# Values and narrow columns of the first mixer in one projection of 304 columns

## The reference

```python
h = rms_norm(x, norm_mix)
proj = h @ w_in
(nsa_q, nsa_kc, nsa_vc, nsa_ks, nsa_vs, nsa_kw, nsa_vw, nsa_g,
 sb_q, sb_k, sb_v, gla_q, gla_k, gla_v, gla_a, gla_g,
 fox_q, fox_k, fox_v, fox_f, gate_logits) = jnp.split(proj, offsets, axis=-1)
...
g = jax.nn.sigmoid(gate_logits).reshape(B, S, G, HPG, 3)               # nsa_g, 24 columns
log_a = jax.nn.log_sigmoid(a_lr @ w_alpha + b_alpha) / GLA_TAU         # gla_a, 16 columns
log_f = jax.nn.log_sigmoid(f_logit + b_f)                              # fox_f, 8 columns
```

## Time and profile before

| | |
|---|---|
| three runs | 1696.88, 1697.82, 1698.09 us; median 1697.82 |
| profiled execution | 1696.86 us, span 1695.1 us, granted clock 0.994 |
| PE | busy 1649.9 us (97%) |
| PEld | 1235.8 us (73%) |
| DVE, ACT, POOL | 929.3 (55%), 712.3 (42%), 155.4 us (9%) |
| chain that ended last | PE 88%, DMA 8% |
| DMA | 420.50 MB, 248 GB/s over the span |
| line 2442 (high parts, 166 of 2048 elements) | 157.0 + 161.0 us, mean 1.92 us |
| line 3279 (low parts, 166) | 192.0 + 197.9 us, mean 2.29 and 2.42 us |

### The profile page before, as it was taken

How to read it: one execution, slowest core, us unless ns; L and a number is a source line. 1 busy time by engine, 2 the same in 40 slices (tenths; PEclk the granted TensorE clock), 3 DMA queues, 4 the chain that set the end, 5 groups by cost and what they waited for, 6 DMA issues and landing times.

```text
span 1695.1 us, 23436 instructions
## 1 busy us (share of the span) xinstructions
PE 1649.9 (97%) x9552; PEld 1235.8 (73%) x9552; DVE 929.3 (55%) x1574; ACT 712.3 (42%) x1065; POOL 155.4 (9%) x140
## 2 busy tenths in 40 slices
PE   8999999988998999999999999999999999999998
PEld 7986434443444389888788888889979878888886
DVE  6684111211111177756579787436756567978744
ACT  4563111111111146645546465323654464555532
POOL 0011000000000012323200000000223310000000
PEclk9999999999999999999999999999999999999999
DMA  8358999999999975444454544546543455445552
GB/s 332 138 223 350 417 414 410 429 428 430 428 429 424 417 278 195 171 162 154 155 201 149 196 169 185 205 149 249 210 163 113 162 174 186 187 155 193 199 208 87
DMA packets 45056, 420.50 MB, mean 248 GB/s; under 512 B 4128, under 2 KB 11936, under 8 KB 18592
## 3 DMA queue, kind: packets, MB, share of 16 engines
q1 hardware_dynamic: 44960, 419.14, 63.1%
HBM read 417.26 MB, written 1.87 MB: 247 GB/s over the span
## 4 chain that ended last, share of the span: by engine, by line
PE 88%; DMA 8%; DVE 1%; issue 1%; ACT 0%; SPq 0%; POOL 0%; POOLq 0%; DVEq 0%; ACTq 0%
PE bank L1387 9%; PE bank L2110 7%; PE bank L1661 6%; DMA work_mem<-in_w 6%; PE bank L1659 5%; PE bank L1660 5%; PE bank L1685 5%; PE bank L1686 5%; PE bank L1691 5%; PE bank L1413 4%; PE bank L2119 4%; PE bank L1588 3%; PE bank L1595 3%; PE bank L1589 3%; DMA wring<-in_w 3%; PE bank L1068 1%
## 5 line engine op out<-in xcount | busy, mean ns | idle before, releaser
L3279 DVE TENSOR_TENSOR w_lo<-wring,w_hi 128x2048 fp32r<-128x2048 f32 x84 | 192.0, 2290 | 110.0 <-ACT w_hi L2442 110.0
L2442 ACT ACTIVATE w_hi_early<-wring 128x2048 fp32r<-128x2048 f32 x82 | 157.0, 1916 | 208.3 <-PE bank L1691 122.0
L2442 ACT ACTIVATE w_hi<-wring 128x2048 fp32r<-128x2048 f32 x84 | 161.0, 1917 | 191.8 <-PE bank L1660 91.8
L3279 DVE TENSOR_TENSOR w_lo<-wring,w_hi_early 128x2048 fp32r<-128x2048 f32 x82 | 197.9, 2416 | 43.8 <-ACT w_hi_early L2442 43.6
L1387 PE MATMUL bank<-wring,gates_mem 128*64 128x512 f32 x720 | 163.2, 595 | 6.3 <-DMA wring<-in_w 6.2
L3193 DVE TENSOR_TENSOR gates_mem<-bank,gates_mem 128x512 f32<-128x512 f32 x32 | 22.1, 691 | 240.8 <-ACT gates_mem L2388 127.2
L1685 PE MATMUL bank<-w_hi_early,mixed 128*128 128x512 f32 x384 | 151.7, 395 | 0.0
L1686 PE MATMUL bank<-w_hi_early,mixed 128*128 128x512 f32 x384 | 149.7, 390 | 0.0
L2110 PE MATMUL bank<-mixed,w_hi 128*128 128x512 f32 x512 | 123.0, 391 | 0.0
L1387 PEld LDWEIGHTS bank<-wring,gates_mem 128*64 128x64 f32 x720 | 52.8, 137 | 94.9 <-issue 93.9
L2110 PEld LDWEIGHTS bank<-mixed,w_hi 128*128 128x128 f32 x512 | 94.0, 188 | 18.1
(11 more groups left out here) (566 smaller groups left out, 3118.2 us busy)
## 6 DMA issues: line engine op xcount, KB each, us to landing
wring<-in_w SPq DMA_DIRECT2D x154, 2048.0 KB, 8.7
work_mem<-in_w SPq DMA_DIRECT2D x32, 2048.0 KB, 17.0
gates_mem<-rel_skew SPq DMA_DIRECT2D x16, 512.0 KB, 8.9
wring<-in_w SPq DMA_DIRECT2D x5, 1024.0 KB, 10.0
work_mem<-in_w SPq DMA_DIRECT2D x2, 1024.0 KB, 15.6
work_mem<-in_w SPq DMA_DIRECT2D x4, 512.0 KB, 18.7
cst<-in_const SPq DMA_DIRECT2D x1, 1224.0 KB, 13.0
prm<-in_prm SPq DMA_DIRECT2D x3, 381.0 KB, 9.3
```

Of the source, the lines that this page charges most:

```text
L2442: act.activation(hi, w, ACT.Copy).then_inc(hi_ready, 2 if h == 1 else 1)
L3279: dve.tensor_tensor(lo, w, hi, ALU.subtract).then_inc(lo_ready, 2 if h == 1 else 1)
```

## The change

The values and the 48 narrow columns become one product of 304 columns, with the token tiles as stationary operand and one PSUM bank for each token tile (`nsa_v` has two jobs, `narrow` has none). It is done by halves of k, with `wide_tokens`: half 4 is now rows 0 to 511 of the chunk's 304 columns, half 5 rows 512 to 1023, 1216 elements per partition each in place of 2048. The two passes stand where `split_tokens` and the narrow product stood: `rope_q` is between them, `hid_cmp(1)` behind them. ScalarE then copies three pieces out of each bank, with the token's factor as scale: the 16 low rank columns, the 32 gate columns, the 256 values. They stand behind the high part of half 6; before, the values were ahead of it. The low rank columns alone are turned, by two transposes, and copied by ScalarE as `a_low`; VectorE's scaling of them goes, and so do the transposes of the gate columns.

```diff
-                        ("nsa_v", 1), ("rope_q", 2), ("narrow", 1), ("hid", 1), ("nsa_f", 1)):
+                        ("nsa_v", TT), ("rope_q", 2), ("hid", 1), ("nsa_f", 1)):
...
-    narrow = gates_mem[0:32, 5376:5376 + S]
+    low_rank = view(gates_mem, 5376, TT, GLA_RANK)
...
-        if c in WIDE_CHUNKS or 26 <= c < 28:
+        if c == 3:
+            k, n, kts, cols = 8, 512, slice(4 * second, 4 * second + 4), slice(0, NSA_V_COLS)
+        elif c in WIDE_CHUNKS or 26 <= c < 28:
...
-        uses = {0: ("nsa_k", 2), 1: ("nsa_q", 1), 2: ("hid", 0), 3: ("narrow", 0), 4: ("hid", 1), 8: ("gates", 1), 9: ("gates", 3),
+        uses = {0: ("nsa_k", 2), 1: ("nsa_q", 1), 2: ("hid", 0), 3: ("nsa_v", 1), 4: ("hid", 1), 8: ("gates", 1), 9: ("gates", 3),
...
-            def split_tokens(j, w, first, cols, used=True):
-
-                free(j, l)
-                for i in range(TT):
-                    out, rows = psum[j.bank][:, i * cols:(i + 1) * cols], slice(i * P, (i + 1) * P)
-                    for k in range(KT):
-                        pe.matmul(out, h_hi[:, k, rows], w[0][:, k, first:first + cols], start=(k == 0), stop=False)
-                        mm = pe.matmul(out, h_lo[:, k, rows], w[0][:, k, first:first + cols], start=False, stop=False)
-                    if used and i == TT - 1:
-                        mm.then_inc(half_used, 1)
-                    for k in range(KT):
-                        mm = pe.matmul(out, h_hi[:, k, rows], w[1][:, k, first:first + cols], start=False, stop=(k == KT - 1))
-                mm.then_inc(bank_full[j.bank], 1)
...
             def wide_tokens(jobs, w, second, low):
 
                 for i, j in enumerate(jobs):
                     if second == 0:
                         free(j, l)
-                    out, rows = psum[j.bank][:, :], slice(i * P, (i + 1) * P)
+                    out, rows = psum[j.bank][:, 0:w[0].shape[2]], slice(i * P, (i + 1) * P)
...
-            split_tokens(layer["nsa_v"][0], half_ready(4), 0, S)
+            wide_tokens(layer["nsa_v"], high_half(4), 0, 4)
             for n in range(2):
                 rope_of("rope_q", n, [q_n[:, 2 * n + t, :] for t in range(2)])
-            w = half_ready(5)
-            j = layer["narrow"][0]
-            free(j, l)
-            for part, x_part in ((w[0], h_hi), (w[0], h_lo), (w[1], h_hi)):
-                for k in range(KT):
-                    mm = pe.matmul(psum[j.bank][:, 0:S], part[:, k, 0:P], x_part[:, k, :],
-                                   start=(x_part is h_hi and part is w[0] and k == 0), stop=(part is w[1] and k == KT - 1))
-                if x_part is h_lo:
-                    mm.then_inc(half_used, 1)
-            mm.then_inc(bank_full[j.bank], 1)
+            wide_tokens(layer["nsa_v"], high_half(5), 1, 5)
             hid_cmp(1)
-            in_sbuf(layer["narrow"], l)
+            in_sbuf(layer["nsa_v"], l)
             j = layer["nsa_f"][0]
             free(j, l)
             for i in range(TT):
-                pe.transpose(psum[j.bank][:, 32 * i:32 * i + 32], narrow[:, i * P:(i + 1) * P], ident[0:32, 0:32])
-            pe.transpose(psum[j.bank][0:4 * KT, P:2 * P], at2["b_gate"], ident).then_inc(bank_full[j.bank], 1)
+                pe.transpose(psum[j.bank][0:GLA_RANK, i * P:(i + 1) * P], low_rank[:, i, :], ident)
...
-            j = layer["nsa_v"][0]
-            full(j, l)
-            for i in range(TT):
-                ins = act.activation(v_n[:, i, :], psum[j.bank][:, i * S:(i + 1) * S], ACT.Copy, scale=in_rstd[:, i:i + 1])
-            ins.then_inc(bank_read[j.bank], 1)
             next_hi(4)
-            j = layer["narrow"][0]
-            full(j, l)
-            act.activation(narrow, psum[j.bank][0:32, 0:S], ACT.Copy)
-            act.activation(a_low, psum[j.bank][32:32 + GLA_RANK, 0:S], ACT.Copy).then_inc(bank_read[j.bank], 1)
+            for i, j in enumerate(layer["nsa_v"]):
+                full(j, l)
+                out, scale = psum[j.bank], in_rstd[:, i:i + 1]
+                act.activation(low_rank[:, i, :], out[:, S + 32:NSA_V_COLS], ACT.Copy, scale=scale)
+                act.activation(fg[:, i, :], out[:, S:S + 32], ACT.Copy, scale=scale)
+                act.activation(v_n[:, i, :], out[:, 0:S], ACT.Copy, scale=scale).then_inc(bank_read[j.bank], 1)
             next_hi(5)
             hid_copy(1)
-            full(layer["nsa_f"][0], l)
-            act.activation(bias_rows[0:4 * KT, :], psum[layer["nsa_f"][0].bank][0:4 * KT, P:2 * P], ACT.Copy)
-            for i in range(TT):
-                ins = act.activation(fg[:, i, :], psum[layer["nsa_f"][0].bank][:, 32 * i:32 * i + 32], ACT.Copy,
-                                     scale=in_rstd[:, i:i + 1])
-            ins.then_inc(bank_read[layer["nsa_f"][0].bank], 1)
+            j = layer["nsa_f"][0]
+            full(j, l)
+            act.activation(a_low, psum[j.bank][0:GLA_RANK, 0:S], ACT.Copy).then_inc(low_rank_ready, 1)
+            act.activation(bias_rows[0:4 * KT, :], psum[j.bank][0:4 * KT, S:S + P], ACT.Copy).then_inc(bank_read[j.bank], 1)
...
-            j = layer["narrow"][0]
-            dve.wait_ge(bank_read[j.bank], j.count(l))
-            dve.tensor_tensor(a_low, a_low, token_factor[0:GLA_RANK, :], ALU.mult).then_inc(low_rank_ready, 1)
-            j = layer["nsa_f"][0]
-            dve.wait_ge(bank_read[j.bank], j.count(l))
+            for j in layer["nsa_v"]:
+                dve.wait_ge(bank_read[j.bank], j.count(l))
```

More of the change, by code:

```diff
@@ L267 @@
 GATE_CHUNKS = (8, 9, 13, 17, 18, 19, 20, 21)
+NSA_V_COLS = S + 32 + GLA_RANK
 WIDE_CHUNKS = (7, 12, 15, 16) + GATE_CHUNKS
@@ L1771, in _ @@
             for i in range(TT):
-                pe.transpose(psum[j.bank][:, 32 * i:32 * i + 32], narrow[:, i * P:(i + 1) * P], ident[0:32, 0:32])
-            pe.transpose(psum[j.bank][0:4 * KT, P:2 * P], at2["b_gate"], ident).then_inc(bank_full[j.bank], 1)
+                pe.transpose(psum[j.bank][0:GLA_RANK, i * P:(i + 1) * P], low_rank[:, i, :], ident)
+            pe.transpose(psum[j.bank][0:4 * KT, S:S + P], at2["b_gate"], ident).then_inc(bank_full[j.bank], 1)
             def compress(kind, n):
@@ L2536, in compress @@
                     act.activation(hid_c.rearrange("p n a b -> p (n a b)"), psum[j.bank][:, 0:8 * N_CMP], ACT.Copy).then_inc(bank_read[j.bank], 1)
-                    j = layer["nsa_f"][0]
-                    act.wait_ge(bank_read[j.bank], j.count(l))
+                    for j in layer["nsa_v"]:
+                        act.wait_ge(bank_read[j.bank], j.count(l))
                     act.activation(fg[:, :, 8:32], fg[:, :, 8:32], ACT.Sigmoid).then_inc(nsa_gate_ready, 1)
```

## The result

Eleven runs of each on one chip: before 1697.82 us (median, 1696.64 to 1699.41), after 1703.49 us (1699.56 to 1704.32), ratio 1.0029 with a 95% interval of 1.0020 to 1.0037. The change makes the kernel 5.7 us slower; forecast were 1698.5 us, and 1701.0 at most. The profiled execution took 1703.73 us, its span 1701.9, 6.8 more than before.

The account below looks back on a forecast made before the run. TensorE was taken to bound the kernel from 600 us on. Its 4.0 us saving turned into two waits, +0.60 us in the first layer and +0.06 in the second, +0.7 on 1697.82: 1698.5 us, range 1695.9 to 1701.0.

Parts of the forecast that it names:

- The work removed: TensorE's values and narrow product: 8.81 us become 6.90 at 0.140 us per 304-column matmul, 1.91 us less in each layer.
- VectorE's 0.17 us: First layer, ahead of `hid_cmp(0)`: a shorter low part of half 4 lets `dup_add` end earlier, saving 0.17 us.
- The new wait: TensorE's transposes wait for ScalarE's six copies, behind half 6 and chunk 5: 2.5 us first layer, 1.8 second.
- the price of the six copies: ScalarE's six copies out of both 304-column banks, behind the high part of half 6: 1.50 us.
- The length of the wait: TensorE idle ahead of the transposes 2.5 and 1.8 us, with half 6 starting at 642.28 and 1185.18 as before.
- The clock: TensorE behind the new gaps: half clock (1.2 GHz in place of 2.4) counted as nothing in the forecast sum.
- the rival at 0.20: TensorE's clock falls behind one gap or both, 1.7 to 3.0 us each: 1700.2 to 1701.5, or 1701.9 to 1704.5; chance 0.20.
- 0.36 of starts: TensorE's transposes come out of an idle gap in both layers and pay a start of 0.18 us each.
- The whole saving arrives: Rival: the transposes do not wait, so all 4.0 us saved on TensorE arrive, 1693.8 us; chance 0.03.
- ScalarE does not hold it as long: Rival: copies cheaper or chunk 5 earlier, half 6 bounds next; gains at most 1.08 and 1.64 us, 1695.1; chance 0.14.

Follow-up runs that it names:

- e8: The changed kernel unaltered, one execution for a second profile: 1069.8 us from the first `hid_cmp(0)` to the end.
- e11: The changed kernel unaltered, one execution for a third profile: 1067.6 us from the first `hid_cmp(0)` to the end.
- e9: Changed kernel with chunk 5 in two transfers, only the two low rank copies ahead of half 6, transposes waiting for these alone: 1694.98 us, ratio 0.9980.
- e1: Changed kernel with ScalarE's copies of the 304 columns moved ahead of the high part of half 6: 1697.68 us, ratio 0.9996.
- e7: The kernel before unaltered, one execution for a second profile: 1064.2 us from the first `hid_cmp(0)` to the end.
- e2: Changed kernel with the slot of chunk 3 given back only behind `hid_cmp(1)`: 1703.12 us, ratio 1.0028.
- e4: Changed kernel with only the first half of chunk 4 transferred, which `hid_cmp(1)` uses twice: 1696.47 us, ratio 0.9987.
- e6: Changed kernel with chunk 5 in two transfers, half 6 waiting for the first alone, copies still behind half 6: 1696.69 us, ratio 0.9990.
- e10: Kernel before with its two copies of values moved behind the high part of half 6: 1699.83 us, ratio 1.0008.

## Why the prediction was wrong

**The work removed: right.** Products of 304 columns start 0.14 us apart, the price that was taken (rows below), and both stretches came out: 10.47 us from `hid_cmp(0)` to `hid_cmp(1)`, forecast 641.27 - 630.68 = 10.59. VectorE's 0.17 us came: the wait ahead of the first `hid_cmp(0)` is 0.20 in place of 0.37.

TensorE's timeline, first layer, after:

```profile
633.95 0.30 PE L1674 MATMUL bank<-w_hi_early,mixed 128*128 128x304 f32 x1
634.09 0.31 PE L1675 MATMUL bank<-w_hi_early,mixed 128*128 128x304 f32 x1
634.23 0.30 PE L1674 MATMUL bank<-w_hi_early,mixed 128*128 128x304 f32 x1
```

**The new wait: right in its place, its order and the price of the six copies** (1.53 us, forecast 1.50).

**The length of the wait: this step failed, above all in the second layer.** I let half 6 start at the same time as in one profile of before, 642.28 and 1185.18, which is 9.47 and 8.93 us behind `hid_cmp(0)`, and gave no range for that. The same step in the six landings of the changed kernel took 9.33 to 10.63. The forecast gaps of 2.5 and 1.8 us came out as 3.33 and 3.72, in e8 as 2.51 and 3.67, in e11 as 2.41 and 3.00. The second profile of before alone, with 9.62 us, would have given 2.5 for the second layer. This is the term that was mis-sized: +1.7 us there on the mean, +0.25 in the first layer. How much of it belongs to the change stays open.

**The clock: the second step that failed.** The sum put the half clock at nothing, and the rival at 0.20 was what happened, in both layers in two of three profiles and in one of them in the third. Its price was too high, 1.7 to 3.0 us each where 1.2 to 1.5 were measured, and its waits were too short. That its time for both, 1701.9 to 1704.5, holds the measured 1703.49 is luck: two errors that cancel. What failed above all is the chance. I had worked out gaps of 2.5 and 1.8 us, and showed one row of 2.70 us that held against two, of 2.71 and 2.90, that did not the earlier trace rows. The profile of before has one more, which I left out:

```profile
467.07 5.35 PE L1413 MATMUL bank<-wring,gates_mem 128*64 128x512 f32 x16 [2.70 <-DMA wring<-in_w]
```

5.35 us for the 16 products is the half clock again, so it was three of four; that is no case for 4 to 1 against, over two gaps. I also took 1.96 us as short enough, and it was not: see the row of 8.78 us above. But no length of gap makes it sure. In the expert stage of e9 the clock held behind 3.34 us:

```profile
528.72 3.65 PE L1423 MATMUL bank<-wring,gates_mem 128*64 128x512 f32 x16 [3.34 <-DMA wring<-in_w]
```

The Trainium skill (TensorE: Matmul & The Clock Gate, Part 1) says that the gate's check runs free of the kernel; 2.70 us with and without a drop, 1.97 and 1.96 us with both outcomes, and 3.34 us without one agree.

**The sum.** Forecast: 3.8 saved and 0.17, against 4.3 of waits and 0.36 of starts, +0.7. Measured: 3.9 saved, against 7.0 of waits, 0.1 of starts and 2.8 of half clock, +6.0 in the two layers of the first profile; +5.7 in the medians. So the forecast missed 2.7 us of waits and all of the clock. In the mean of the three profiles it is 6.2 of waits and +5.0 in all.

**"The whole saving arrives", at 0.03, and "ScalarE does not hold it as long"** (1695.1, a gain of 2.7): neither is what the changed kernel does. But e9 shows that the second was right about the next bound: in e9 the low part of half 6 is what comes last. That e9 gains 2.7 us by its trace as well proves less: there half 6 starts behind the second low rank copy and not behind the landing of its chunk.

## What to carry to other kernels

When work is taken off the bounding engine, look up who feeds it next and what stands ahead of that work in the feeder's list: a copy queued behind a transfer waits for the transfer, ready or not. Put ahead only the pieces that are waited for (e9), since the order of that list alone was worth 5.8 us here (e1). And where a forecast leaves TensorE idle for as long as rows show a half clock behind, count all such rows and give the clock their share as its chance; take the landing time of a transfer as a range over several profiles, not as the value of one.

## What the runs showed of the hardware

- From the end of `hid_cmp(0)`, where chunk 5 (2 MB) is asked for, to the start of half 6 it took 8.93 to 10.63 us over ten cases (before, after, e7, e8, e11), behind the same queue; between executions of one kernel it moved by 0.7 and 0.9 us.
- Ahead of the transposes, the half clock came behind 5 of 6 gaps of 2.4 to 3.7 us of the changed kernel, both of e2's (3.37 and 2.98), and none of e4's, e6's and e10's, of 0.6 to 1.7 us. From 200 us on, in all 14 profiles and all stages, it came behind none of 71 gaps of 1.3 to 1.8 us, 13 of 45 of 1.95 to 1.98, 30 of 42 of 2.64 to 2.72, and 14 of 20 of 2.82 to 3.72; the six of 2.82 to 3.34 us that held were all in the expert stage.
- A drop cost 1.2 to 1.5 us here: some 14 products of 256 columns started 0.21 us apart in place of 0.12.
- With 1 MB less in the queue ahead of chunk 5, half 6 started 2.4 and 2.7 us earlier than in the first profile of the changed kernel, 2.1 earlier than on the mean of its three (e4). With a signal for the first half of chunk 5 it was 1.9 and 2.0, or 1.5 against that mean (e6).
- Products of 304 columns started 0.14 us apart, of 256 columns 0.12.
